# First layers of a gated hybrid decoder step in another order, and two of them by seven products of quarters for eight

## The chip, the cores and the metric

The kernel runs on one core of a Trainium2 chip. The metric is the device time of one execution in microseconds, the median of the runs shown.

## What is computed

One step of a one-layer decoder trunk: a chunked gMLP mixer and a sparse attention mixer side by side, merged by sigmoid gates, then layer norm, a mixture of experts and another layer norm. There are 1024 prompt tokens and 8 sample tokens, 1032 columns in all, each of width 1024. The change touches the projections from x and the first branch:

```python
u, v, q, *kv_new, g_nsa, g_a, g_b = split_projection(xp, w_in[l])
vn = layer_norm(gelu(v), ln_g, ln_b)                 # v, in chunks of 128 positions
a = gelu(u) * (einsum(tril(w_s), vn) + b_s)          # per group of 128 channels
mix = (sigmoid(g_a) * (a @ w_pa) + sigmoid(g_b) * (o @ w_pb)) @ w_o
```

u, v, q, g_a and g_b are 1024 x 1024 layers over the 1032 columns; a @ w_pa (branch a) is one more.

## The kernel before

All values are fp32. A product is made of three passes (`PASSES`, line 184): each operand is split into a high part of the rounded type fp32r and a low part, the rest, and high x high, high x low and low x high are summed in PSUM. The split is always one cast on ACT (`high`) and one subtraction on DVE (`low`).

A 1024 x 1024 layer in turned form is 8 tiles of 128 output channels. A tile (`Tiles.products`, line 245) is 3 thirds of 344 columns x 8 k x 3 passes = 72 matmuls, each of which loads its own 128x128 weights. Its 512 KB of weights are loaded by SP into one of two buffers when the tile before the last is done, then cast by ACT and subtracted by DVE.

The order: `load_and_turn_x` (line 399) loads x in 9 tiles (8 of 128 tokens and the 8 samples), turns each on PE, and casts and subtracts it; the value weights (4 MB) are loaded behind x. `gmlp_values` (line 495) splits the value weights in 8 k, projects v for each token tile (48 matmuls of 512 columns), applies gelu, normalises on DVE (lines 473 to 484), mixes with the turned W_s (`mix(t)`, 8 small matmuls behind the next tile's products) and adds b_s (`keep(t)`) into `m.aT`. At its end PE goes from `mix(7)` to tile 0 of u, and then to `mix(8)`, the samples. `gmlp_gate` (line 652) does u: gelu on ACT, times aT on DVE, and the split of a. `merge_first` (line 706) does the first gate and branch a in turn, 16 tiles. `second_gate` (line 770) does g_b and spills its sigmoid to DRAM (`gate_b`), while the kv weights are loaded and two of their eight k split; `project_kv` and `project_q` follow. Each engine runs its instructions strictly in the order that these functions are called in; what crosses engines waits on semaphores. The lines before the prediction's steps, from `gmlp_values`:

```python
        pe.wait_ge(fw.u.s_lo, 1)
        pe.wait_ge(s_gelu, TT)
        pe.wait_ge(s_kept, TT - 1)
        fw.u.products(0, m.x_parts, 3).then_inc(fw.s_uproj, 1)
        mix(TT)
```

Everything behind the projections (compression, attention, merge, output, router, experts, last norm) is the same in both kernels.

## Time and profile before

| | |
|---|---|
| median of 3 runs | 1965.28 us (1965.21 to 1966.11) |
| the profiled execution's own time | 1966.16 us |
| its span in the trace | 1964.4 us |
| PE busy | 96% of the span |
| DVE, ACT, POOL busy | 54%, 44%, 24% |
| granted TensorE clock, mean | 0.976 |

The span is what the trace covers of one execution; the time is 1.8 us longer, which lies around it. PE stands for TensorE's matmuls, PEld for its weight loads (beside PE), DVE for VectorE, ACT for ScalarE, POOL for GpSimd, SP for the queue that issues the transfers. A busy share is an average over stages; what an engine waits for is read in the stage itself. A matmul's duration is longer than the distance to the next one, since they are pipelined; what a matmul costs is that distance.

### The profile page before, as it was taken

How to read it: one execution, taken by the hardware profiler on the slowest of the kernel's cores; microseconds unless marked ns; L12 is line 12 of the kernel's file. 1: busy time of each engine (PE TensorE's matmuls, PEld its weight loads, DVE VectorE, ACT ScalarE, POOL GpSimd, SP SyncE). 2: the span in 40 equal slices, each digit the busy share in tenths (PEclk: the TensorE clock that was granted, in tenths of full speed). 3: DMA queues.
4: the chain of work that ended last, by engine and by line, in shares of the span. 5: the costliest groups of instructions: out<-in, count | busy, mean ns of one | idle time of the engine just before them, and what ended most of it. 6: DMA issues, size and time to landing. Idle time of an engine off the chain costs nothing.

```text
span 1964.4 us, 31223 instructions
## 1 busy us (share of the span) xinstructions
PE 1886.6 (96%) x11538; PEld 1700.4 (87%) x11539; DVE 1065.5 (54%) x1530; ACT 862.0 (44%) x1455; POOL 467.1 (24%) x640
## 2 busy tenths in 40 slices
PE   7999999999999999999999999999977999999996
PEld 5889999999999987898888988998856888888883
DVE  5543211101112347888888888744557587644756
ACT  4112211112211256778877887520022576544754
POOL 0000000000000025545555554101211244322433
PEclk9999999999999987999999999999987999999998
DMA  6011111132213410000000000434153798877864
GB/s 225 1 33 45 46 52 43 49 117 86 92 39 85 132 35 9 1 1 2 1 1 1 2 1 2 153 95 152 78 201 131 270 390 295 305 276 236 320 205 181
DMA packets 98516, 215.65 MB, mean 110 GB/s; under 512 B 23130, under 2 KB 71810, under 8 KB 92226
## 3 DMA queue, kind: packets, MB, share of 16 engines
q1 hardware_dynamic: 90946, 188.90, 26.7%
q0 software_dynamic: 7456, 25.17, 5.2%
q8 instruction: 79, 1.29, 0.3%
q14 instruction: 35, 0.29, 0.0%
HBM read 181.88 MB, written 34.26 MB: 110 GB/s over the span
## 4 chain that ended last, share of the span: by engine, by line
PE 51%; DVE 6%; ACT 3%; issue 2%; POOL 1%; DVEq 0%; ACTq 0%; POOLq 0%
PE ps L2562 20%; PE ps L1652 6%; PE ps L2233 5%; PE ps L1631 4%; PE ps L251 3%; PE ps L1606 2%; PE ps L1608 2%; DVE small L1706 1%; PE ps L2550 1%; ACT region_w L1795 1%; DVE region L1738 1%; PE ps L2602 1%; PE ps L1598 1%; PE ps L1585 1%; PE ps L2219 1%
## 5 line engine op out<-in xcount | busy, mean ns | idle before, releaser
L1706 DVE TENSOR_REDUCE small<-ps 128x1 f32<-128x640 f32 (+7 forms) x256 | 180.0, 704 | 44.6 <-PE ps L1598 42.0
L1806 ACT CAST turned_high<-ps 128x512 fp32r<-128x512 f32 (+2 forms) x304 | 154.7, 531 | 86.4 <-PE ps L1631 85.9
L1730 DVE TENSOR_TENSOR turned_low<-ps,turned_high 128x512 fp32r<-128x512 f32 (+2 forms) x304 | 173.4, 613 | 8.9 <-ACT turned_high L1806 8.4
L1864 POOL TENSOR_SCALAR region_w<-region_w,small,gates 128x640 f32<-128x640 f32 (+7 forms) x172 | 133.3, 785 | 166.3 <-DVE small L1710 165.8
L1652 PE MATMUL ps<-turned_high,value_stacks 128*128 128x256 f32 (+1 forms) x608 | 152.6, 286 | 10.5 <-DVE region L1738 10.4
L1606 PE MATMUL ps<-key_stacks,query_stacks 128*128 128x256 f32 (+3 forms) x384 | 142.7, 372 | 6.4 <-ACT region L1795 2.3
L2562 PE MATMUL ps<-down_parts,hidden_parts 128*128 128x512 f32 x576 | 139.6, 399 | 3.5 <-DVE down_parts L2858 3.5
L1652 PE MATMUL ps<-turned_low,value_stacks 128*128 128x256 f32 (+1 forms) x608 | 142.6, 279 | 0.0
L2562 PE MATMUL ps<-gate_parts,rows_parts 128*128 128x512 f32 x552 | 133.2, 397 | 3.1 <-DVE rows_parts L2870 3.1
L2562 PEld LDWEIGHTS ps<-down_parts,hidden_parts 128*128 128x128 f32 x576 | 108.5, 192 | 25.4 <-DVE down_parts L2858 3.7
L1652 PEld LDWEIGHTS ps<-turned_high,value_stacks 128*128 128x128 f32 x608 | 115.4, 190 | 16.4 <-issue 15.2
L2562 PE MATMUL ps<-up_parts,rows_parts 128*128 128x512 f32 x552 | 128.9, 389 | 0.0
L1126 POOL MEMSET region<- 128x1096 f32 x1 | 1.1, 1098 | 534.7 <-issue 534.7
L1795 ACT ACTIVATE region_w<-ps,small 128x640 f32<-128x640 f32 (+7 forms) x172 | 121.7, 708 | 10.6 <-DVE small L1706 7.2
L2562 PEld LDWEIGHTS ps<-gate_parts,rows_parts 128*128 128x128 f32 x552 | 103.3, 191 | 24.3 <-issue 3.3
L1608 PE MATMUL ps<-key_lows,query_stacks 128*128 128x256 f32 (+3 forms) x384 | 122.7, 331 | 0.0
L2562 PEld LDWEIGHTS ps<-up_parts,rows_parts 128*128 128x128 f32 x552 | 103.6, 188 | 21.5
L1652 PEld LDWEIGHTS ps<-turned_low,value_stacks 128*128 128x128 f32 x608 | 115.4, 190 | 0.0
L1631 PE MATMUL ps<-ident,region_w 128*128 128x128 f32 x708 | 107.0, 278 | 3.9 <-POOL region_w L1864 3.5
L2233 PE MATMUL ps<-w_out_high,y_parts 128*128 128x512 f32 (+1 forms) x288 | 91.0, 392 | 0.0
L2858 DVE TENSOR_TENSOR down_parts<-region_w,down_parts 128x2048 fp32r<-128x2048 f32 x32 | 72.0, 2289 | 33.9 <-ACT down_parts L2667 32.5
L2858 DVE TENSOR_TENSOR gate_parts<-region_k,gate_parts 128x2048 fp32r<-128x2048 f32 x32 | 71.9, 2288 | 31.4 <-ACT gate_parts L2667 31.4
(466 smaller groups left out, 4983.5 us busy)
## 6 DMA issues: line engine op xcount, KB each, us to landing
region_k<-in_w_gate SPq DMA_DIRECT2D x16, 2048.0 KB, 9.0
region_k<-in_w_up SPq DMA_DIRECT2D x16, 2048.0 KB
region_w<-in_w_down SPq DMA_DIRECT2D x16, 2048.0 KB, 12.8
region_w<-in_w_in SPq DMA_DIRECT2D x20, 512.0 KB, 3.9
gate_b<-region_w SPq DMA_DIRECT2D x8, 516.0 KB, 4.2
region_w<-gate_b SPq DMA_DIRECT2D x8, 516.0 KB, 4.1
region_k<-in_x_prompt SPq DMA_DIRECT2D x8, 512.0 KB, 6.7
region_w<-in_w_in SPq DMA_DIRECT2D x4, 1024.0 KB, 14.3
```

The source lines that it names most:

```text
L1606: nc.tensor.matmul(out, qs[:, g, tile], k1[:, a, g, k0:k0 + w], start=True, stop=False, skip_group_check=True)
L1608: nc.tensor.matmul(out, qs[:, g, tile], k2[a][:, g, k0:k0 + w], start=False, stop=True, skip_group_check=True)
L1631: last = nc.tensor.transpose(m.ps[:, turn_bank(G), r * P:(r + 1) * P], part, m.ident[:])
L1652: last = nc.tensor.matmul(out, vs[:, a, g, b, :], parts[x][:, r * P:r * P + w], start=(a == 0 and r == 0 and x == 0), stop=False, skip_gro ...
L1706: nc.vector.tensor_reduce(nmax[:, n % 4:n % 4 + 1], sc, AX.X, ALU.max, negate=True).then_inc(s_max, 1)
L1730: nc.vector.tensor_tensor(lo, m.ps[:, turn_bank(G), 0:w], hi, ALU.subtract).then_inc(s_lo, 1)
L1795: nc.scalar.activation(probs(H, t), sc, ACT.Exp, bias=nmax[:, n % 4:n % 4 + 1], accum_out=sums[:, H % 4, t:t + 1]).then_inc(s_exp, 1)
L1806: nc.scalar.copy(hi, m.ps[:, turn_bank(G), 0:w]).then_inc(s_hi, 1)
L1864: nc.gpsimd.tensor_scalar(probs(H, t), probs(H, t), rec[:, H % 4, t:t + 1], m.gates[:, 2 * p + t, col:col + 1], ALU.mult, ALU.mult).then_i ...
L2233: last = nc.tensor.matmul(m.ps[0:n, 2 * (t % 2) + c, :], yparts[:, t % 2, a, k, 0:n], wparts[b][:, k, c * 512:(c + 1) * 512], start=(k == ...
L2562: last = nc.tensor.matmul(out, x[:, a, k, :], w[:, b, k, columns], start=(k == 0 and i == 0), stop=(k == count - 1 and i == 2))
L2858: nc.vector.tensor_tensor(wparts[q][:, 1, part], raw_third(m, q)[:, part], wparts[q][:, 0, part], ALU.subtract).then_inc(s_lo[q], 1)
```

## The change

*Order.* The first gate g_a comes first (`first_gate`): its tile 0 is done by thirds between the turnings of x (when three, six and nine x tiles are split; PE turns one tile more before each of the first two), and its sigmoid is spilled to DRAM (`gate_a`). Then u and g_b (`second_layers`), gelu(u) spilled too (`gelu_u`), then the values. `gmlp_values` now reads gelu(u) back per token tile, multiplies it in `keep(t)`, splits a in 8 pieces (`PIECES`: four of the first third of the columns, two each of the second and third; `high_a`, `low_a`), and ends with branch a's tiles 0 and 1 by thirds. `merge_first` is the rest of branch a, with the first gate read back. The second gate's stage is gone, and with it the work beside which the kv weights were loaded and split.

*Seven products.* u and g_b are 8 rounds; round r makes output tiles q and q + 4 of a layer. Weights and x are taken as 2 x 2 quarters: A11, A12, A21, A22 are 512 x 128 of weights, x11 to x22 are 512 x 516 of x. With S1 = A21 + A22, S2 = S1 - A11, S3 = A11 - A21, S4 = A12 - S2 and t1 = x12 - x11, t2 = x22 - t1, t3 = x22 - x12, t4 = x21 - t2, the products are 1 A11 x11, 2 A12 x21, 3 S4 x22, 4 A22 t4, 5 S1 t1, 6 S2 t2, 7 S3 t3, and the four quarters of the output are 1+2, 1+6+5+3, 1+6+7+4 and 1+6+7+5. A product is 4 k x 3 passes x 2 halves of 258 columns = 24 matmuls; two in turn have the same weights. Sums of products with the same bank are made in PSUM, the others by an ACT copy and a DVE addition. The sums of x are made once on DVE beside the first gate; those of the weights in each round (`combine`).

The core of the diff:

```diff
+    def combine(self, dve, r):
+
+        a11, a12, a21, a22, s1, s2, s4 = (self.raw[r % 2][:, q] for q in range(7))
+        for i in range(2):
+            dve.wait_ge(self.s_in[r % 2][i], 16 * (r // 2 + 1))
+        self.sum(dve, s1, a21, a22, ALU.add)
+        self.sum(dve, a21, a11, a21, ALU.subtract)
+        self.sum(dve, s2, s1, a11, ALU.subtract)
+        self.sum(dve, s4, a12, s2, ALU.subtract)
 
...
+        def first_chunk(c):
+            if c == 0:
+                pe.wait_ge(w.s_lo, 1)
+            pe.wait_ge(s_kept, FIRST_TURNS[c] + 1)
+            last = w.chunk(0, m.x_parts, c, c)
+            if c == NC3 - 1:
+                last.then_inc(s_proj, 1)
...
+            if t - 1 in FIRST_TURNS:
+                first_chunk(FIRST_TURNS.index(t - 1))
+        first_chunk(NC3 - 1)
+        for n in range(1, LAYERS):
+            pe.wait_ge(w.s_lo, n + 1)
+            if n >= 2:
+                pe.wait_ge(s_func, n - 1)
+            w.products(n, m.x_parts, 4 * (n % 2)).then_inc(s_proj, 1)
...
+        for n in range(1, LAYERS):
+            w.low(dve, n)
+            if n == 1:
+                dve.wait_ge(fw.s_stack, 2)
+                fw.sums.sum3(dve)
+            if n == 2:
+                fw.sums.sum2(dve)
+                fw.sums.low(dve, fw.sums.t3, fw.sums.raw3, 1)
+            if n == 3:
+                fw.sums.sum4(dve)
+                fw.sums.low(dve, fw.sums.t2, fw.sums.raw2, 2)
+            if n == 4:
+                fw.sums.sum1(dve)
+            if n == 5:
+                fw.sums.low(dve, fw.sums.t4, fw.sums.raw4, 3)
+                fw.sums.low(dve, fw.sums.t1, fw.sums.raw1, 4)
+            if n == 6:
+                fw.half.combine(dve, 0)
+                fw.half.low(dve, 0, 0)
...
+    order = [("1", 0)]
+    for r in range(NR):
+        order += [("2", r), ("6", r), ("5", r), ("7", r)] + ([("1", r + 1)] if r + 1 < NR else []) + [("3", r), ("4", r)]
...
+        def out(done, r, dst, src, sem):
+            sp.wait_ge(done, r + 1)
+            sp.dma_start(dst, src).then_inc(sem, 16)
+
+        for r in range(NR):
+            dst, q = spills[r // HK], r % HK
+            if r == 0:
+                for b in range(2):
+                    sp.wait_ge(fw.s_spill[b], 16 * KT // 2)
+                sp.wait_ge(fw.s_xproj, KT)
+                fw.load_half(sp, 1)
+            elif r + 1 < NR:
+                sp.wait_ge(s_prod, nth["4", r - 1])
+                fw.load_half(sp, r + 1)
+            else:
+                sp.wait_ge(s_prod, nth["4", r - 1])
+                for i in range(3):
+                    fw.load_v(sp, i)
+            out(s_f11, r, dst[q][:, left], first, s_o11)
+            out(s_f22, r, dst[q + HK][:, right], third, s_o22)
+            if r + 1 == NR:
+                sp.wait_ge(s_o22, 16 * NR)
+                fw.load_v(sp, 3)
+            out(s_f12, r, dst[q][:, right], second, s_o12)
+            out(s_f21, r, dst[q + HK][:, left], fourth, s_o21)
...
+            for k in range(HK):
+                for i, (a, b) in enumerate(PASSES):
+                    stationary = (w.hi, w.lo)[a][r % 2][:, q, k, :]
+                    for c in range(2):
+                        last = nc.tensor.matmul(m.ps[:, bank + c, 0:HW // 2], stationary,
+                                                x[b][:, k, c * (HW // 2):(c + 1) * (HW // 2)],
+                                                start=(start and k == 0 and i == 0), stop=(stop and k == HK - 1 and i == 2),
+                                                skip_group_check=True)
+            last.then_inc(s_prod, 1)
...
+        product1(0)
+        for r in range(NR):
+            if r == 0:
+                pe.wait_ge(fw.s_xfunc, KT)
+                pe.wait_ge(x.s_low, 4)
+            else:
+                pe.wait_ge(s_11, r)
+            product("2", r, BANK_C, A12, x.x21, True, True)
+            pe.wait_ge(w.s_lo, 2 * r + 2)
+            pe.wait_ge(s_c1, r + 1)
+            product("6", r, bank_a(r), S2, x.t2, False, False)
+            if r >= 1:
+                pe.wait_ge(s_12, r)
+            product("5", r, BANK_B, S1, x.t1, True, False)
+            pe.wait_ge(s_c2, r + 1)
+            product("7", r, bank_a(r), S3, x.t3, False, False)
+            if r + 1 < NR:
+                product1(r + 1)
+            pe.wait_ge(s_22, r + 1)
+            product("3", r, BANK_B, S4, x.x22, False, True)
+            pe.wait_ge(s_c3, r + 1)
+            product("4", r, bank_a(r), A22, x.t4, False, True)
...
+        w.high(act, 0, 1)
+        keep(0, "1", first, s_c1, s_o11)
+        for r in range(NR):
+            if r + 1 < NR:
+                w.high(act, r + 1, 0)
+            apply(r, s_11, first, s_f11)
+            keep(r, "6", second, s_c2, s_o12)
+            if r + 1 == NR:
+                for k in range(2):
+                    fw.high_v(act, k, nth["5", r])
+            keep(r, "7", third, s_c3, s_o22)
+            if r + 1 < NR:
+                w.high(act, r + 1, 1)
+                keep(r + 1, "1", first, s_c1, s_o11)
+            apply(r, s_22, third, s_f22)
+            if r + 1 == NR:
+                for k in range(2, 4):
+                    fw.high_v(act, k, nth["5", r])
+            apply(r, s_12, second, s_f12)
+            act.wait_ge(s_prod, nth["4", r])
+            if r >= 1:
+                act.wait_ge(s_o21, 16 * r)
+            nc.scalar.activation(halves(fourth), two(bank_a(r)), funcs[r // HK]).then_inc(s_f21, 1)
+        for k in range(4, KT):
+            fw.high_v(act, k, nth["5", NR - 1])
...
+        w.low(dve, 0, 1)
+        for r in range(NR):
+            add(r, "2", s_c1, first, BANK_C, s_11)
+            if r + 1 < NR:
+                w.combine(dve, r + 1)
+                w.low(dve, r + 1, 0)
+            else:
+                for k in range(2):
+                    fw.low_v(dve, k)
+            add(r, "5", s_c3, third, BANK_B, s_22)
+            if r + 1 == NR:
+                for k in range(2, 4):
+                    fw.low_v(dve, k)
+            add(r, "3", s_c2, second, BANK_B, s_12)
+            if r + 1 < NR:
+                w.low(dve, r + 1, 1)
+        for k in range(4, KT):
+            fw.low_v(dve, k)
...
+            if t >= 1:
+                sp.wait_ge(s_gated, t)
+            sp.dma_start(gu[:, :, 0:rows_of(t)], m.gu_dram.rearrange("k p c -> p k c")[:, :, span(t)]).then_inc(s_u, 16)
...
         def turn_ws():
             pe.wait_ge(s_c, 80)
+            pe.wait_ge(fw.s_hfunc[1], NR)
...
-        pe.wait_ge(fw.u.s_lo, 1)
+        pe.wait_ge(w.s_lo, 1)
         pe.wait_ge(s_gelu, TT)
+        pe.wait_ge(s_rows, 1)
+        for c in range(2):
+            for k in range(KT):
+                pe.wait_ge(fw.s_al, k // 2 + 1 if c == 0 else 5 + k // 4)
+                w.term(0, m.a_parts, c, k, c)
+        mix(TT)
+        pe.wait_ge(w.s_lo, 2)
         pe.wait_ge(s_kept, TT - 1)
-        fw.u.products(0, m.x_parts, 3).then_inc(fw.s_uproj, 1)
-        mix(TT)
+        for c in range(2):
+            w.chunk(1, m.a_parts, c, 3 + c)
+        pe.wait_ge(fw.s_al, 8)
+        for n in range(2):
+            w.chunk(n, m.a_parts, 2, 3 * n + 2).then_inc(fw.s_fproj, 1)
...
             nc.vector.tensor_tensor(m.aT[:, :, span(t)], src, add, ALU.add).then_inc(s_kept, 1)
+            dve.wait_ge(s_u, 16 * (t + 1))
+            dve.wait_ge(s_kept, t + 1)
+            nc.vector.tensor_tensor(m.aT[:, :, span(t)], m.aT[:, :, span(t)], gu[:, :, 0:n], ALU.mult).then_inc(s_gated, 1)
...
             if t == TT:
+                for n in range(2):
+                    low_a(dve, n)
                 dve.wait_ge(s_lows, 1)
                 v = vn[t].rearrange("p (a c) -> p a c", a=2)
                 nc.vector.tensor_tensor(v, v, m.ps[0:NB, 0:2, :], ALU.add).then_inc(s_rows, 1)
+                for n in range(2, 4):
+                    low_a(dve, n)
+                keep(TT - 1)
             dve.wait_ge(s_gelu, t + 1)
             normalise(nc, dve, vn[t], rows_of(t), stats, mv, rstd, gain, bias,
                       s_stat, s_mv, s_rstd, s_norm, t, s_v)
...
+            if t == TT:
+                for n in range(4, 6):
+                    low_a(dve, n)
+                w.low(dve, 1)
         keep(TT)
...
+        sp.wait_ge(fw.s_vmix, TT)
+        fw.load_a(sp, 1)
+        sp.wait_ge(fw.s_vnormal, NT9)
+        sp.wait_ge(fw.s_vgated, NT9)
+        sp.dma_start(sa, m.sga_dram[0]).then_inc(s_gate, 16)
+        sp.wait_ge(fw.s_vout, 16)
+        for k in range(4):
+            fw.load_kv(sp, k)
+        for n in range(2, KT):
+            sp.wait_ge(s_proj, n - 1)
+            fw.load_a(sp, n)
...
 
 
     @block.sync
     def _(sp):
-        sp.wait_ge(fw.s_gbproj, KT - 1)
+        sp.wait_ge(fw.s_fproj, KT)
+        for k in range(4, KT):
+            fw.load_kv(sp, k)
         fw.load_q(sp, 0)
...
```

What stands on DVE in a round. Before, in the second gate's and in u's tile, DVE had one subtraction of weights a tile (`gb_low` or `u_low`; u also its multiplication and a's subtraction):

```order
L696 TENSOR_TENSOR region<-region,region_k 128x1032
L698 TENSOR_TENSOR a_low<-region,a_high 128x1032
L243 TENSOR_TENSOR u_low_83<-small,u_high_82 128x1024
L696 TENSOR_TENSOR region<-region,region_k 128x1032
L698 TENSOR_TENSOR a_low<-region,a_high 128x1032
```

Now, one round (line 837 adds products 2, 5 and 3, line 373 combines the next round's weights, line 367 makes their low parts, first of A11 and A12, then of the five others):

```order
L837 TENSOR_TENSOR small<-small,ps 128x516
L373 TENSOR_TENSOR region_w<-region_w 128x512 x4
L367 TENSOR_TENSOR half_w_low_119<-region_w,half_w_high_117 128x1024
L837 TENSOR_TENSOR region_k<-region_k,ps 128x516
L837 TENSOR_TENSOR small<-small,ps 128x516
L367 TENSOR_TENSOR half_w_low_119<-region_w,half_w_high_117 128x2560
```

The combination is between product 2 of this round and product 1 of the next.

The second place is DVE at the end of the value stage (the normalisation of the samples is the six rows from BN_STATS on 8 partitions). Before:

```order
L640 TENSOR_TENSOR region_k<-region_k,ps 8x1024
L475 BN_STATS small<-region_k 8x6
L476 BN_STATS small<-region_k 8x6
L478 BN_AGGR small<-small 8x2
L480 TENSOR_SCALAR region_k<-region_k,small 8x1024
L482 TENSOR_TENSOR region_k<-region_k 8x1024
L484 TENSOR_TENSOR region_k<-region_k 8x1024
L634 TENSOR_TENSOR region<-ps,region_k 128x8x128
L243 TENSOR_TENSOR u_low_85<-region_w,u_high_84 128x1024
L634 TENSOR_TENSOR region<-ps,region_k 128x8x8
```

Now, from a's first pieces (`a_low`, line 914) on:

```order
L914 TENSOR_TENSOR a_low<-region,a_high 128x2x344 x2
L1063 TENSOR_TENSOR region_w<-region_w,ps 8x1024
L914 TENSOR_TENSOR a_low<-region,a_high 128x2x344 x2
L1052 TENSOR_TENSOR region<-ps,region_w 128x8x128
L1055 TENSOR_TENSOR region<-region,small 128x8x128
L861 BN_STATS small<-region_w 8x6
L862 BN_STATS small<-region_w 8x6
L864 BN_AGGR small<-small 8x2
L866 TENSOR_SCALAR region_w<-region_w,small 8x1024
L868 TENSOR_TENSOR region_w<-region_w 8x1024
L870 TENSOR_TENSOR region_w<-region_w 8x1024
L914 TENSOR_TENSOR a_low<-region,a_high 128x4x344 x2
```

The pieces of the second third (128x4x344) stand behind `keep(7)` (two rows now) and the samples' normalisation.

## Rows read from the trace of the kernel before

**Rows 1.** The page, part 1: busy us, share, instructions
```profile
PE 1886.6 (96%) x11538; PEld 1700.4 (87%) x11539; DVE 1065.5 (54%) x1530; ACT 862.0 (44%) x1455; POOL 467.1 (24%) x640
```

**Rows 2.** Stretches: us, each engine's busy us, PEclk, DMA share, GB/s
```profile
0.00:24.00 24.00, 10.66 (x72) 9.00 (x73) 11.36 (x13) 12.15 (x15) 2.23 (x14) 0.96 0.93 357
132.00:232.00 100.00, 99.92 (x627) 97.63 (x625) 38.25 (x35) 25.73 (x25) 0.77 (x2) 0.98 0.18 48
232.00:413.00 181.00, 181.00 (x1154) 181.00 (x1153) 30.51 (x25) 28.25 (x27) 0.00 (x0) 1.00 0.17 47
413.00:503.50 90.50, 90.50 (x578) 90.50 (x577) 10.42 (x9) 15.08 (x15) 0.00 (x0) 1.00 0.34 113
```

**Rows 3.** Timeline of PE in attention, a run of 256-column matmuls: start, duration
```profile
1099.82 0.28 PE L1652 MATMUL ps<-turned_high,value_stacks 128*128 128x256 f32 x1
...
1100.40 0.28 PE L1652 MATMUL ps<-turned_low,value_stacks 128*128 128x256 f32 x1
```

**Rows 4.** Timeline of the start
```profile
6.53 1.01 ACT L459 CAST x_high<-ps 128x1024 fp32r<-128x1024 f32 x1 [4.46 <-PE ps L448]
...
8.94 1.07 PE L448 MATMUL ps<-ident,region_k 128*128 128x128 f32 x8 [0.74 <-DVE x_low L467]
...
19.49 0.63 PE L448 MATMUL ps<-ident,small 8*128 8x8 f32 x8 [0.74 <-DVE x_low L467]
...
24.07 0.79 PE L582 MATMUL ps<-w_v_high,x_high 128*128 128x512 f32 x1 [3.95 <-DVE w_v_low L622]
```

**Rows 5.** Stretches around two falls of PE's clock, columns as in rows 2
```profile
24.00:28.00 4.00, 3.93 (x9) 3.14 (x10) 4.00 (x5) 4.00 (x5) 0.00 (x0) 0.50 1.01 317
28.00:32.00 4.00, 4.00 (x17) 3.21 (x16) 3.96 (x4) 2.67 (x3) 0.00 (x0) 0.90 0.84 292
...
152.00:156.00 4.00, 4.00 (x18) 4.00 (x17) 2.88 (x3) 2.00 (x2) 0.00 (x0) 0.61 0.13 38
```

**Rows 6.** Groups by form: busy us, mean ns of one, idle before
```profile
L2858 DVE TENSOR_TENSOR down_parts<-region_w,down_parts 128x2048 fp32r<-128x2048 f32 x32 | 72.0, 2289 | 33.9 <-ACT down_parts L2667 32.5 <-issue 1.3
L2667 ACT CAST down_parts<-region_w 128x2048 fp32r<-128x2048 f32 x32 | 59.4, 1906 | 10.0 <-DMA region_w<-in_w_down 9.2 <-issue 0.3
L2877 DVE TENSOR_TENSOR region<-region,ps 128x512 f32<-128x512 f32 x24 | 16.4, 684 | 37.8 <-PE ps L2562 37.8
L2688 ACT ACTIVATE region<-ps 128x512 f32<-128x512 f32 x24 | 14.3, 597 | 50.1 <-PE ps L2562 39.6 <-PE ps L2627 10.4
L243 DVE TENSOR_TENSOR gb_low<-region_w,gb_high 128x1024 fp32r<-128x1024 f32 x8 | 9.8, 1224 | 63.5 <-ACT gb_high L238 63.5
L238 ACT CAST gb_high<-region_w 128x1024 fp32r<-128x1024 f32 x8 | 8.4, 1050 | 18.0 <-DMA region_w<-in_w_in 18.0
```

**Rows 7.** Single transfers issued at 232.34, 232.77, 137.29, 493.62, 413.36: us to landing
```profile
region_w<-in_w_in SPq DMA_DIRECT2D x1, 512.0 KB, 4.0
...
region_w<-in_w_in SPq DMA_DIRECT2D x1, 512.0 KB, 5.3
...
region_w<-in_w_branch_a SPq DMA_DIRECT2D x1, 512.0 KB, 6.5
...
gate_b<-region_w SPq DMA_DIRECT2D x1, 516.0 KB, 2.7
...
region<-in_w_in SPq DMA_DIRECT2D x1, 1632.0 KB, 6.5
```

**Rows 8.** Timeline at the value stage's end
```profile
136.03 1.95 PE L563 MATMUL ps<-region_k 128*128 128x128 f32 x16
...
137.29 1.06 SPq L233 DMA_DIRECT2D region_w<-in_w_branch_a  x1
...
142.34 0.68 DVE L475 BATCH_NORM_STATS2 small<-region_k 8x6 f32<-8x512 f32 x1 [3.86 <-ACT region_k L613]
...
146.89 1.21 DVE L484 TENSOR_TENSOR region_k<-region_k 8x1024 f32<-8x1024 f32 x1
```

**Rows 9.** A stretch at the attention's beginning, columns as in rows 2
```profile
725.00:730.00 5.00, 5.00 (x25) 4.78 (x24) 4.89 (x5) 3.30 (x6) 0.00 (x0) 0.50 0.00 0
```

669 lines of the change are left out of this document (374 added, 295 removed).

## The prediction

> **What bounds the kernel now.** I read the page first: PE is busy 96% of the span [rows 1], so time is won by giving PE less to do or by closing its gaps. Then the table of stretches [rows 2]: the layers that the change touches lie between 24 and 504 us, and PE is busy without a break in 132:232, 232:413 and 413:503.5. 1152 of the 344-column matmuls (16 tiles of 72) fill 232:413, 181.0 us, so one costs 157.1 ns. DVE and ACT have 10 to 38 us of work in each of these stretches: they are cover. The start is a gap: 24 us with PE busy for 10.66. Next I read the start's order [rows 4], the durations of the two helpers [rows 6], the landings [rows 7], the tail of the value stage [rows 8] and PE's clock [rows 5, 9].
>
> **The change, part by part.**
>
> *Columns.* Layers u and the second gate are 16 of the 344-column tiles, 1152 matmuls, 181.0 us. Seven products of 24 matmuls in 8 rounds are 1344 matmuls of 258 columns. No row has 258; a run of six matmuls of 256 columns has five steps in 0.58 us, 116 ns each [rows 3], with two columns more 117, and from the 344-column side 157.1 less 86 columns at 2.4 GHz is 121.3 ns. I take 119.5, between the two: 160.6 us. Ends: 157.2 and 163.0. **-20.4 us** (-23.8 to -18.0).
> There are 192 matmuls more, so the part of a matmul's cost that does not shrink with its columns decides: rows 2 and 3 together (41 ns for 88 columns, 37 at 2.4 GHz) leave 9 to 14 ns for it. The Trainium skill (TensorE: Matmul & The Clock Gate, Back-to-back issue gap) gives about 81 ns at 128 columns and 131 at 512 for a stream of weight loads and matmuls, a far larger fixed part: on its line this term would be +6 us.
>
> *Start.* Before, PE turns x until 20.1, then waits for split value weights; its first product starts at 24.07 [rows 4] and runs at 1.2 GHz until about 28.8 (granted 0.50 in 24:28, 0.90 in 28:32 [rows 5]), so 2.4 us more are lost: effectively it starts at 26.4. Now a third of the first gate's tile 0 follows once three x tiles are split. x tile 0 is split on ACT from 6.53 [rows 4]; one weight load lies between x tiles 0 and 1, with one cast (1.05) and one subtraction (1.22) [rows 6]. With the tile's cycle of 1.76 us (turn 1.07, cast 1.01, subtract 1.22, two banks): third one 12.5 to 16.3, second 20.9 to 24.7, last 28.2 to 32.0. A tile is 72 x 0.157 = 11.3 us, so the effective start is 20.7: **-5.7 us** (-6 to -3, the low end if the clock falls here as it did at 20:24).
> The other seven gate tiles run back to back if low(n) is there in 11.3 us: landing 4.0, cast 1.05, cast of a 2064-column sum 1.9, subtraction 2.3, low 1.2, in all 10.5 [rows 6, 7]. Nothing added, 0.8 us of slack.
>
> *First round.* The 2560-column split starts only after the last sigmoid (1.0): cast 2.36, subtraction 2.82 (from 2048 columns in 1.91 and 2.29 [rows 6]) end at 6.3 us; products 1 and 2 cover 5.75. Then ACT is blocked by the cast of weights 1, which are loaded after the last gate spill (4.0 us) and land at 9.3; with a table load and two copies, product 7 waits 0.9. **+1.4** (0.5 to 3).
>
> *Middle rounds.* This is the tightest place. From the end of product 4, which frees a buffer, to the product 1 that reads what is then loaded into it, products 2, 6, 5 and 7 pass: 4 x 24 x 0.1195 = 11.5 us. Against it: fourth activation 0.6, two issues after a spill 0.4, landing of the second of two loads 5.7 (the pair at 232: second issued 0.43 later, 5.3 to land [rows 7]), 0.3 behind the spill's data, four sums of 512 columns 0.69 each, a subtraction of 1024 columns 1.22: 11.1. **0** (up to +0.5 in each of 6 rounds, +3).
>
> *Last round.* No product 1 stands between 7 and 3: product 3 waits for copy 7 (0.6) and addition 5 (0.7): **+1.4**. The value weights are split beside it: the first two before product 3, four more pairs of cast and subtraction within 6.6 us of its end, while PE takes 1.4 us for each k of value tile 0 (6 matmuls of 512, 157 plus 168 columns at 2.4 GHz, 0.227 each), so they are hidden; if they weren't, up to +2. The mixing weights and constants are loaded only when the last spill is out (0.6 + 2.3 us), 4.0 for the first and 1.3 for each of three more: at 11.0, when tile 0 is over at 10.9. **+0.3** (0 to 3).
>
> *Value tail: the dearest added wait.* Zero is the start of mix(7), 136.03 before [rows 8]. Then u tile 0 followed without a gap, since it needs only x. Now branch a follows, which needs a. PE waits for the sample rows (after two casts, two subtractions and the addition: 3.85) from 1.95: 1.9 us. The first third is done at 7.6. The second third needs a pieces 4 and 5, and DVE does these behind keep(7) (two passes of 1.22, to 8.0) and the samples' normalisation, 142.34 to 148.10, 5.76 us [rows 8], though only 8 rows: 13.8, plus a 1376-column subtraction 1.6 = 15.4. PE idles 7.8 us. All else in this tile is in time. Such an idle stretch also costs clock: before, after 3.9 idle us, it ran at 0.50 for 4.7 busy us, 2.4 us lost [rows 4, 5]. 1.9 + 7.8 + 2.4 = **+12.1 us** (8 to 14).
>
> *Branch a, third tile.* Its load waits for the first of the two last chunks; landing 3.9, cast, subtraction 6.2 against a chunk of 3.8: **+2.5** (1.5 to 4). Later tiles have 11.3 us for it.
>
> *kv weights.* Before, all eight k were loaded and two of them split beside the second gate, and PE waited 0.7 us at its end. Now k 4 to 7 are loaded after the last a tile: 4.5 us for the first pair (one of 1632 KB took 6.5 [rows 7], half of it counts some 2 us less), cast, subtraction: 6.6 against 4.6: **+1.4** (0 to 3).
>
> The projections of kv and q, and all behind them, are as before. Branch a's 8 tiles, the gate's 8 and the value tiles have the same matmuls.
>
> Sum: -20.4 - 5.7 + 1.4 + 0 + 1.4 + 0.3 + 12.1 + 2.5 + 1.4 = **-7.0 us**. The profiled execution took 1966.16, so 1959.2 on its own terms. The median of the three runs is 0.9 lower than it: I predict **1958.3**. A measurement of this kernel can tell about 0.2%, 3.9 us, from no change.
>
> **Rivals.**
> *The rounds wait for weights (0.14), which ends on the other side.* Place: DVE's combination of the next round's weights, ahead of product 1, in the six middle rounds. For: 0.4 us of slack only. With three loads queued before, the third took 6.5 from its own issue and 7.5 from the first [rows 7, 8], and its issue alone took SP 1.06 for 0.4 [rows 8]; two spills of 258 KB precede the pair now. With 7.5 for 6.0, 0.6 more for the issue and 0.8 for 0.69 a sum, the chain is 13.6 against 11.5: six times 2.1 are +12.6 on the forecast, 1970.9. It decides from 1.2 us a round. Against: a spill of 516 KB behind nothing landed in 2.7 [rows 7], so its data are short.
> *The clock moves elsewhere (0.15, half to either side).* The attention's beginning runs at 0.50 with PE mostly busy [rows 9], from 721 to 759; nothing in the code fixes its ends, and all of it shifts. A stretch like that in 152:156 (0.61 over 4 us [rows 5], 1.6 us lost) more or less is the smallest step; three of them make it 1953.5 or 1963.
> *The tail is cheaper (0.09).* The clock does not fall, and DVE gets to piece 4 earlier than I count, or the waits at a's third tile and at kv are covered: 4 + 2 + 1.4 less, 1951.
> *A matmul's fixed part is larger than rows 3 show (0.01).* Runs of 256 columns are short there, and here two matmuls in turn have the same weights, each with its own load. At 134.7 ns for 258 columns (181.0 / 1344) the columns give nothing; at 140 they cost 7.2: 1986. Against: both widths measured differ by the clock's price of their columns. The skill's line (the section named above) gives 98 ns for 258 and 109 for 344, by which the whole would be 1984.7; rows 2 and 3 have 157 for 344 and speak against it.
> That the change doesn't do what it says: seven products are in the code, each with its own weight load; no matmul is dropped elsewhere.
>
> **How the numbers follow.** Forecast 0.61, of which 0.10 ends within 0.2%. Of the rounds' 0.14, 0.06 are slower, 0.07 within and 0.01 faster; the clock 0.07 within, 0.08 faster; the tail 0.09 faster; the fixed part 0.01 slower. Faster 0.51 + 0.01 + 0.08 + 0.09 = 0.69, same 0.10 + 0.07 + 0.07 = 0.24, slower 0.07. The bounds of the columns (-3.4 to +2.4), the tail (-4 to +2), start (+2.6), rounds (+3) and constants (+2.7) don't all fall on one side: 1949 to 1968.
>
> **What would show it.** Matmuls of 258 columns start 0.1195 us apart; PE starts its first 344-column matmul at 12 to 13 us; each middle round is 20.1 us with no wait for the weights' low parts; PE idle for 7 to 8 us in the second third of branch a's first tile, released by DVE's a_low, and 0.5 in the clock behind it; 2.5 us before a's third tile; about 2 us in kv tile 0. I am wrong if the rounds take over 21 us, if the tail pause is missing, or if the attention's half-rate stretch changes by more than 7 us.

## The result, and the profile after

The changed kernel takes **1971.12 us** (median of 13 runs, 1966.62 to 1976.28), the kernel before 1965.6 in 13 runs beside them (1963.05 to 1967.85): ratio **1.0029**, 95% interval 1.0020 to 1.0039. It is slower by 5.5 us; 7.0 less was forecast, and the range ended at 1968. Its runs also spread over 10 us instead of 5. The profiled execution took 1972.23 (span 1970.1), 6.1 more than that of before.

The page, part 1, of the changed kernel, answers [rows 1]:

```profile
PE 1873.3 (95%) x11730; PEld 1683.7 (85%) x11731; DVE 1147.1 (58%) x1601; ACT 898.1 (46%) x1502; POOL 471.1 (24%) x640
```

PE has 13 us less to do than before in 192 more matmuls, and the span is 6 longer: what was saved came back as waiting. The stretches say where (columns as in [rows 2]; first gate, seven products, values, tail, branch a, kv and q, compression):

```profile
31.00:112.40 81.40, 81.40 (x520) 81.40 (x519) 42.45 (x25) 21.76 (x18) 0.00 (x0) 1.00 0.32 98
112.40:279.40 167.00, 163.42 (x1346) 162.17 (x1345) 71.07 (x71) 64.22 (x77) 0.00 (x0) 1.00 0.38 118
279.40:397.00 117.60, 113.86 (x554) 92.14 (x553) 63.70 (x72) 17.69 (x19) 7.48 (x17) 0.99 0.22 66
397.00:435.00 38.00, 27.26 (x160) 26.48 (x160) 19.31 (x20) 9.04 (x9) 0.76 (x2) 0.91 0.37 113
435.00:503.30 68.30, 68.01 (x433) 68.01 (x434) 15.49 (x14) 6.90 (x7) 0.00 (x0) 1.00 0.26 81
503.30:666.30 163.00, 161.16 (x957) 157.33 (x957) 32.61 (x40) 24.26 (x33) 0.00 (x0) 1.00 0.28 79
666.30:739.80 73.50, 66.93 (x409) 60.80 (x407) 33.19 (x92) 32.49 (x73) 11.32 (x21) 0.89 0.29 87
```

PE's rows that carry a wait, in brackets the idle time and its releaser (timeline of PE):

```profile
118.82 0.52 PE L757 MATMUL ps<-x_sum_high,half_w_high 128*128 128x258 f32 x2 [0.42 <-DVE half_w_low L367]
...
273.56 0.51 PE L757 MATMUL ps<-x_high,half_w_high 128*128 128x258 f32 x2 [1.48 <-DVE region_k L837]
...
293.37 1.29 PE L953 MATMUL ps<-ident,region_w 128*128 128x128 f32 x8 [2.57 <-DMA small<-in_gmlp_ws]
...
398.04 0.40 PE L250 MATMUL ps<-a_high,branch_a_high 128*128 128x344 f32 x1 [2.21 <-DVE region_w L1063]
409.06 0.66 PE L250 MATMUL ps<-a_high,branch_a_high 128*128 128x344 f32 x1 [7.01 <-DVE a_low L914]
435.29 0.43 PE L250 MATMUL ps<-a_high,branch_a_high 128*128 128x344 f32 x1 [2.98 <-DVE branch_a_low L244]
...
510.00 0.45 PE L1205 MATMUL ps<-w_kv_high,x_high 128*128 128x408 f32 x1 [1.74 <-DVE w_kv_low L459]
...
710.44 3.61 PE L1472 MATMUL ps<-ident,region 128*128 128x128 f32 x16 [2.65 <-DMA region<-in_cache_kv]
```

All but the last lie where the change altered the code or the order of the loads. Three of the waits are followed by a stretch in which PE's clock is granted 0.50, though PE is busy again (the stretch with the wait, then the one behind it; before each the clock is at 1.00 or 0.99):

```profile
291.00:294.10 3.10, 0.73 (x7) 0.73 (x8) 0.00 (x0) 0.86 (x1) 0.00 (x0) 1.00 1.00 347
294.10:297.50 3.40, 3.40 (x12) 2.72 (x11) 2.75 (x5) 0.00 (x0) 1.11 (x1) 0.50 0.02 5
402.00:406.80 4.80, 0.05 (x1) 0.00 (x0) 3.73 (x6) 0.00 (x0) 0.76 (x2) 1.00 0.12 7
406.80:413.60 6.80, 4.54 (x16) 4.54 (x17) 4.24 (x4) 1.04 (x1) 0.00 (x0) 0.50 0.30 82
707.50:710.60 3.10, 0.45 (x3) 0.16 (x2) 0.00 (x0) 0.46 (x1) 0.00 (x0) 0.99 0.26 83
710.60:714.00 3.40, 3.40 (x17) 3.40 (x17) 1.39 (x2) 0.59 (x1) 0.00 (x0) 0.51 0.00 0
```

They cost 1.6, 2.2 and 1.6 us beyond the waits (each step in them less the median step of its shape at full rate). No such stretch follows the waits of 2.21 us at 398.04 and of 2.98 at 435.29, so the length of a wait alone doesn't tell whether the clock falls.

The last wait is in compression, the stage behind q, code that the change does not touch. Before, the same turn of the keys starts with no wait:

```profile
706.58 1.91 PE L1160 MATMUL ps<-ident,region 128*128 128x128 f32 x16
```

PE needs the last of 16 pages there, and SP's loop issues them one by one. SP's issues in that loop, before and after (start, time from the first to the end of the last issue, count):

```profile
685.07 19.25 SPq L395 DMA_DIRECT2D region<-in_cache_kv  x13
```

```profile
685.00 23.61 SPq L532 DMA_DIRECT2D region<-in_cache_kv  x14
```

Less the last issue itself (0.36) that is 12 turns in 18.9 us before and 13 in 23.25 after: **1.58 and 1.79 us a turn**, the same instructions. The transfers themselves land as quickly (2.3 and 2.2 us). A turn is ten instructions of SP, and the extra stands in two of its steps: from the loop's branch to the next instruction 0.27 us for 0.16, and from that one to the next 0.19 for 0.10.

### The profile page after: what moved, and what is told of

It reads as the page before. It is cut to its first block, busy times and chain, and to the rows that moved or that the text cites. A ratio compares the mean times of both kernels' runs of the same rounds, so it can differ in the third digit from the quotient of the medians.

```text
span 1970.1 us, 31853 instructions
## 1 busy us (share of the span) xinstructions
PE 1873.3 (95%) x11730; PEld 1683.7 (85%) x11731; DVE 1147.1 (58%) x1601; ACT 898.1 (46%) x1502; POOL 471.1 (24%) x640
## 4 chain that ended last, share of the span: by engine, by line
PE 45%; DVE 6%; ACT 3%; issue 3%; DMA 3%; POOL 1%; DVEq 0%; ACTq 0%; POOLq 0%; SPq 0%
PE ps L2874 15%; PE ps L1964 6%; PE ps L2545 5%; PE ps L1943 4%; PE ps L250 3%; DMA region_w<-in_w_down 2%; PE ps L1918 2%; PE ps L1920 2%; DVE small L2018 1%; DVE region L2050 1%; PE ps L2914 1%; ACT region_w L2107 1%; PE ps L1910 1%; PE ps L2862 1%; DVE down_parts L3170 1%
## 5 line engine op out<-in xcount | busy, mean ns | idle before, releaser
L1964 PEld LDWEIGHTS ps<-turned_high,value_stacks 128*128 128x128 f32 x608 | 115.4, 190 | 16.5 <-issue 15.3
L3170 DVE TENSOR_TENSOR down_parts<-region_w,down_parts 128x2048 fp32r<-128x2048 f32 x32 | 72.0, 2288 | 34.2 <-ACT down_parts L2979 32.9
L1918 PEld LDWEIGHTS ps<-key_stacks,query_stacks 128*128 128x128 f32 x384 | 74.0, 193 | 14.8 <-issue 9.9
```

What stands on the lines that cost most here:

```text
L1918: nc.tensor.matmul(out, qs[:, g, tile], k1[:, a, g, k0:k0 + w], start=True, stop=False, skip_group_check=True)
L1964: last = nc.tensor.matmul(out, vs[:, a, g, b, :], parts[x][:, r * P:r * P + w], start=(a == 0 and r == 0 and x == 0), stop=False, skip_gro ...
L3170: nc.vector.tensor_tensor(wparts[q][:, 1, part], raw_third(m, q)[:, part], wparts[q][:, 0, part], ALU.subtract).then_inc(s_lo[q], 1)
```

## The experiments

Each was compared with the kernel before on the same chip, but not all on one chip. Ratios are therefore compared, not medians. The difference of two ratios is uncertain by about 0.15%, 3 us (an estimate from the two intervals). Medians and ratios:

| kernel | median us (runs) | ratio to before, 95% |
|---|---|---|
| changed | 1971.12 (13) | 1.0029 (1.0020 to 1.0039) |
| changed, once more (e11_changed_again) | 1974.43 (5) | 1.0043 (1.0030 to 1.0056) |
| low first (e1_low_first) | 1976.85 (6) | 1.0064 (1.0052 to 1.0076) |
| tail (e2_tail) | 1967.12 (12) | 1.0012 (1.0000 to 1.0023) |
| constants (e3_consts) | 1970.93 (7) | 1.0029 (1.0018 to 1.0041) |
| loop head (e4_head16) | 1968.33 (12) | 1.0017 (1.0006 to 1.0028) |
| tail + constants (e9_tail_consts) | 1963.72 (11) | 0.9989 (0.9978 to 0.9999) |
| tail + head (e10_tail_head) | 1961.63 (12) | 0.9982 (0.9972 to 0.9992) |
| all three (e5_all) | 1958.25 (5) | 0.9963 (0.9950 to 0.9977) |
| all three, more (e8_more) | 1958.65 (5) | 0.9965 (0.9952 to 0.9979) |
| the same, product 4 first (e12_four_first) | 1957.29 (7) | 0.9967 (0.9951 to 0.9983) |
| order without seven products (e6_plain) | 1977.71 (4) | 1.0064 (1.0048 to 1.0079) |
| before, SP padded (e7_before_pad) | 1969.02 (10) | 1.0022 (1.0012 to 1.0031) |

**1. Is the page loop slower because of where it lies?** Two runs from opposite sides. In the changed kernel the loop's head is pinned:

```diff
-    with sp.Fori(first, end) as i:
+    with m.nc.Fori(first, end, engines=bass.OrderedEngineSet([sp.engine]),
+                   head_slot=head and {sp.engine: head}) as i:
...
-            load_pages(m, io, sp, m.R1, slice(256, 512), 4096, si.s_page)
+            load_pages(m, io, sp, m.R1, slice(256, 512), 4096, si.s_page, head=16)
```

> Only the place in memory of SyncE's loop over the 16 page loads of the compress stage is changed: its first instruction is put at a fixed slot (16) of an instruction block; the instructions are the same. In the kernel before a turn of this loop takes 1.58 us, in the changed one 1.79, with the extra 0.21 us in the two steps right behind the loop's branch. Theory A (placement of the loop's head, moved by the extra SyncE instructions of the change): a turn takes 1.5 to 1.6 us, the last page lands 3 us earlier, TensorE's 2.8 us wait at 707.5 and the half-rate stretch behind it (1.6 us) go, time 1966 to 1968. Theory B (contention, or the page table read): a turn stays at 1.79 us and the time at 1971.

In the kernel before, 55 idle instructions push it on:

```diff
+        for i in range(55):
+            sp.nop(f"pad{i}")
         sp.wait_ge(s_xl, 1)
```

> The kernel before with 55 idle SyncE instructions (as many as the change adds to SyncE ahead of that point) put where SyncE waits anyway, ahead of the page loop; nothing else. If the place of the loop's head in memory makes a turn 1.79 instead of 1.58 us: the last page lands 3 us later than in the kernel before, TensorE waits 2.6 to 3 us at about 706, the clock falls behind it, and the time is 3 to 5 us above before (1968 to 1970). Rival: the loop keeps its 1.58 us (what slowed it is something else that the change does), time as before.

SP's issues, pinned (changed kernel) and padded (kernel before):

```profile
686.88 24.05 SPq L532 DMA_DIRECT2D region<-in_cache_kv  x16
```

```profile
682.30 25.83 SPq L395 DMA_DIRECT2D region<-in_cache_kv  x15
```

Pinned: 23.7 / 15 = 1.58 us a turn, and PE turns the keys at 713.10 with no wait. Padded: 25.47 / 14 = 1.82 (the extra stands at the branch, 0.28 for 0.16, and behind the read of the page's number, 0.30 for 0.20), and the wait is there in the kernel before:

```profile
709.92 1.96 PE L1162 MATMUL ps<-ident,region 128*128 128x128 f32 x16 [3.14 <-DMA region<-in_cache_kv]
```

By the ratios the padded kernel is 0.22% (4.3 us) slower than before, clear of 1 by its interval. The pinned one is 2.4 us faster than the changed one (5.1 against its second series), and the first of these is within the uncertainty. Its profiled execution shows why so little is seen: from kv's start to the end it takes 1461.6 us, the changed kernel 1466.8, but kv starts 5.1 us later (508.37 for 503.28), with more stretches at half rate ahead of it, in code that is the same (part 3 has them).

That the place of the loop sets its turn is shown from both sides, and contention as the cause of the slower turn is out: the pinned kernel issues the same transfers. Counted in the traces, SP runs 264 instructions ahead of the loop in the kernel before and 303 in the one without seven products (part 5), both with the fast turn, and 319 in the padded and 321 in the changed one, both with the slow turn. The pinned one has 322 and the fast turn: not the number as such, but where it puts the loop. Which boundary the loop meets is not shown. The Trainium skill (Runtime: NRT & Kernel Launch, Instruction fetch mechanics) says that most engines fetch instructions in blocks of 256 and hold two, and that a taken branch to code outside them has to wait for a fetch. No run here tells whether the 0.2 us a turn is such a wait.

**2. The tail: one order, two ways.** First VectorE's order alone:

```diff
-                for n in range(2, 4):
+                for n in range(2, 6):
                     low_a(dve, n)
                 keep(TT - 1)
...
-                for n in range(4, 6):
-                    low_a(dve, n)
                 w.low(dve, 1)
```

> VectorE writes pieces 4 and 5 of a_low (first two of the second 344-column third) before it adds and gates value tile 7; nothing else changes. In the changed kernel TensorE waits 7.2 us for piece 4. Theory A (the wait is VectorE's queue, and it is passed on): piece 4 lands near 401.7 us, so that wait goes, but normalising the sample rows ends no earlier than before (the same 13 us of VectorE work stand ahead of it), and the mix of the sample rows, which is next on TensorE, waits 6 to 7 us instead; start of the key-value products 503.3 us within 1 us, time within 0.2% of the changed kernel's 1971. Theory B (the wait is piece 4 alone): the mix does not wait, the half-rate stretch at 407 goes too, time 1962 to 1964.

PE's next wait, and the clock behind it:

```profile
412.46 3.58 PE L968 MATMUL ps<-small,region_w 8*128 8x8 f32 x16 [5.62 <-DVE region_w L870]
419.50 0.65 PE L250 MATMUL ps<-a_high,branch_a_high 128*128 128x344 f32 x1 [3.46 <-DVE branch_a_low L244]
```

```profile
411.50:425.10 13.60, 9.18 (x35) 9.09 (x36) 5.58 (x6) 3.62 (x3) 0.00 (x0) 0.50 0.45 134
```

The wait was handed on, as theory A says: 5.6 us at the mix of the sample rows. But a second one followed it, 3.5 for the second weight tile, which the changed kernel doesn't have: 9.1 us of waiting instead of 7.0. PE was at half rate for 13.6 us instead of 6.8 (how much of that is this execution's own is open, see part 3), and kv starts at 508.38, not at 503.3. The kernel is 0.35% slower than the changed one (0.21% against its second series). Both theories missed that.

Then the order of all four queues:

```diff
+            if t == TT:
+                sp.wait_ge(s_mix, TT)
+                fw.load_a(sp, 1)
             if t >= 1:
                 sp.wait_ge(s_gated, t)
...
-        mix(TT)
         pe.wait_ge(w.s_lo, 2)
         pe.wait_ge(s_kept, TT - 1)
-        for c in range(2):
-            w.chunk(1, m.a_parts, c, 3 + c)
+        w.chunk(1, m.a_parts, 0, 3)
+        mix(TT)
+        w.chunk(1, m.a_parts, 1, 4)
...
-                keep(TT - 1)
             dve.wait_ge(s_gelu, t + 1)
-            normalise(nc, dve, vn[t], rows_of(t), ...)
+            moments(nc, dve, vn[t], rows_of(t), ...)
+            if t == TT:
+                for n in range(4, 6):
+                    low_a(dve, n)
+                w.low(dve, 1)
+            scale(nc, dve, vn[t], rows_of(t), ...)
...
+        keep(TT - 1)
         keep(TT)
```

`moments` and `scale` are the two halves of `normalise`, cut ahead of its wait for GpSimd's deviation; the load of a's second tile stood behind the sample rows' output.

> The end of the value stage in another order: branch a's second weight tile is loaded as soon as the mix of tile 7 is done, ahead of the wait for the sample rows; VectorE takes the moments of the sample rows, then a_low pieces 4 and 5 and the weight tile's low part, then scales the rows; TensorE puts the first third of the second tile ahead of the mix of the sample rows and the second third behind it. If the tail's waits are what the trace says (7.2 + 2.2 of half rate, TensorE idle with work that could run), 6 to 9 us of it go: start of the key-value products 494 to 497 us instead of 503.3, and the time 1962 to 1965. Rival: whatever the tail gives back is lost behind it, since the page loads of the compress stage set the start of attention; then the wait there grows and the time stays within 0.2% of 1971.

The 7.0 us wait is gone, 1.8 remain at another place (and 3.4 us at half rate behind it):

```profile
421.01 0.43 PE L250 MATMUL ps<-a_high,branch_a_high 128*128 128x344 f32 x1 [1.77 <-DVE a_low L918]
```

In this execution the values began 2.8 us later than in the changed kernel's (282.21 for 279.46). Half of that is a fall of PE's clock in the first gate, behind a wait of 1.91 us that the changed kernel has too, there without a fall:

```profile
29.30:32.70 3.40, 3.06 (x11) 3.07 (x12) 3.37 (x5) 1.51 (x2) 0.00 (x0) 0.51 0.00 0
```

Kv starts at 501.19, not at 494 to 497 as expected: 4.8 us are won between. By the ratios the time fell by 3.3 us (6.1 against the second series). The rival is out: the wait in compression is 2.9 us, for 2.7 in the changed kernel.

**3. The constants.**

```diff
-        for out in fw.s_hout:
-            sp.wait_ge(out, 16 * NR)
-        sp.dma_start(ws, io["gmlp_ws"].rearrange("l g t s -> t (l g) s")).then_inc(s_c, 16)
+        sp.wait_ge(fw.s_hprod, 7 * NR)
+        sp.dma_start(ws, io["gmlp_ws"].rearrange("l g t s -> t (l g) s")).then_inc(s_ws_in, 16)
...
+        for out in fw.s_hout:
+            sp.wait_ge(out, 16 * NR)
         with nc.allow_non_contiguous_dma(reason="one weight per group"):
...
-            pe.wait_ge(s_c, 80)
+            pe.wait_ge(s_ws_in, 16)
```

> The mixing weights, gain, bias and spatial bias are loaded as soon as the last of the seven-product rounds is done (about 279.5 us) instead of behind the four spills (284.8), and TensorE's turn of the mixing weights waits for their load alone, not for all five constants. If the 2.7 us wait at 290.6 and the half-rate stretch 294.1 to 297.5 (1.6 us) come from these loads: both go, value tile 1 starts near 291.5 instead of 294.3 and runs at full rate, time 1966 to 1967.5. Rival: the clock stretch does not come from the wait and stays (time 1968.5), or the load is late anyway because the last piece of the value weights is in the queues (wait stays over 1.5 us, time 1970).

The wait and the fall of the clock at 294 are gone, as expected:

```profile
290.00:296.00 6.00, 6.00 (x32) 4.99 (x31) 2.27 (x4) 1.02 (x1) 0.98 (x1) 1.00 0.54 188
```

Yet by the ratios the time is that of the changed kernel's first series (and 2.8 us below its second). In the profiled execution the tail has three stretches at half rate, where the changed kernel's has one:

```profile
395.70:399.10 3.40, 3.40 (x12) 3.40 (x13) 3.30 (x4) 3.29 (x3) 0.00 (x0) 0.50 0.00 0
405.90:412.70 6.80, 6.00 (x21) 6.00 (x22) 3.47 (x3) 1.05 (x1) 0.00 (x0) 0.50 0.29 82
416.20:419.60 3.40, 3.40 (x14) 3.40 (x13) 2.26 (x2) 2.35 (x2) 0.00 (x0) 0.50 0.77 243
```

It would be easy to read this as the clock taking back what the edit gave. But the pinned kernel's profile has three stretches in the same place too, at 408.9, 419.1 and 439.6, and its code is the changed kernel's up to there:

```profile
419.10:422.50 3.40, 3.40 (x13) 3.40 (x14) 1.89 (x3) 2.58 (x2) 0.00 (x0) 0.50 0.50 151
439.60:443.00 3.40, 3.40 (x14) 3.40 (x14) 1.55 (x2) 1.05 (x1) 0.00 (x0) 0.50 0.51 166
```

How often the clock falls in the tail thus varies from execution to execution, and one profile of each kernel can't say that the constants' edit caused it. From the start of the values to kv this execution takes 221.6 us, the two profiled ones of the changed kernel 223.8 and 223.7.

**4. Do the three add?** The pairs and the triple.

> The reordered tail and the early constants, the page loop left where the change puts it. Alone, the tail was worth 3.3 us of median, the constants nothing and the loop's place 2.4, but all three together 13. Theory A (two idle stretches close to each other draw the clock down further, so the constants pay only when the tail's waits are gone): 1962 to 1963.5, that is the three together less the 4.4 us of the page loop's wait and its half-rate stretch. Theory B (the three are independent, and the sum of all was a draw of the clock): 1967 to 1968.

> The reordered tail and the page loop's head at slot 16, the constants left as in the changed kernel. Theory A (as for the run before): the constants' wait (2.7) and its half-rate stretch (1.6) are back, and with them falls of the clock behind them: 1962 to 1964.5. Theory B: 1965.5, the sum of the two alone.

> The changed kernel once more, unchanged, on the same chip and against the same runs of the kernel before as the two runs above, for the spread: 1966 to 1976 with a median of 1971, 0.3% above before. If it comes out below 1968, the comparisons with it across chips have to be read with that.

> The three edits that each left work order intact but for one place, together: the reordered end of the value stage, the mixing weights loaded early, the page loop's head at slot 16. If their gains add: against the changed kernel's 1971.1, 4 us (tail) and 2.5 to 3 us (loop) and 0 to 4 us (constants; alone it removed the wait but the clock fell elsewhere): 1961 to 1965, level with or below the kernel before (1965). Rival: the clock takes back what the waits give; then the trace shows more than three half-rate stretches between 290 and 450 us and the time stays at 1966 to 1968.

The pairs came out at 1963.7 and 1961.6, where theory B had 1967 to 1968 and 1965.5. But theory B's figures rest on the first series of the changed kernel (1.0029). With the second (1.0043), a plain sum of the single edits gives 0.9998 and 0.9986 for the pairs and 0.9972 for all three, and the measured 0.9989, 0.9982 and 0.9963 have these within their intervals. So it is **not shown whether the three add**; the first series alone says that they give more together.

By the ratios the constants are worth 4.5 us once the tail is in order and 3.7 with the loop pinned too; on the tail as the change made it, between nothing and 2.8. The loop's place is worth 5.9 on the tail's kernel, 5.1 on tail and constants. What doesn't hang on these differences is the whole: all three are 7.3 us faster than the kernel before (0.9963, interval 0.9950 to 0.9977) and 13 faster than the changed kernel. In its profiled execution kv starts at 496.80 and the rest takes 1459.7 us (before: 503.67 and 1460.7; changed: 503.28 and 1466.8). The second series of the changed kernel came out higher, 1.0043; what is told here against the changed kernel uses the first unless said.

**5. The two halves of the change.**

```diff
-LAYERS = KT
+LAYERS = 3 * KT
...
-        col = COL_GA + n * P
+        col = (COL_GA, 0, COL_GB)[n // KT] + n % KT * P
...
-            second_layers(nc, m, io, fw, block)
```

> The new order without the seven products: u and the second gate come from sixteen more plain 344-column weight tiles (1152 products) in the same loop as the first gate, still ahead of the values; all behind is as in the changed kernel. This prices the two halves of the change apart. From the traces: sixteen tiles at 11.3 us are 181, the seven-product stage took 167.0, so this kernel should be 12 to 16 us slower than the changed one (1983 to 1987), the order alone 18 to 22 us worse than before, and the seven products worth about 14. Rival: the waits at the end of the seven-product stage and the constants' wait belong to the seven products and go with them; then 7 to 9 us slower (1978 to 1980).

In its profiled execution the values start at 294.72 instead of 279.46 and kv at 514.94 instead of 503.28 (before: 503.67). So **the order alone costs some 11 us by the start of kv, and the seven products give some 11 back** (both some 10 without the 1.3 that PE's slower start took in this execution, see the last section): 15.3 up to the values, less 3.6 behind them, mostly the constants (a wait of 2.7 is 1.3 here, with no fall of the clock behind it). This kernel also loads and splits the value weights in another place, beside the last four of its tiles. The median is only 6.6 above the changed kernel, below both expectations: SP has another number of instructions here, the page loop runs at 1.57 us a turn, and the 4.4 us behind it are absent. With them added (an estimate) it would be 11, still below the 12 to 16 that were expected.

**6. Two smaller places, then a third.**

```diff
             if r + 1 < NR:
                 w.combine(dve, r + 1)
                 w.low(dve, r + 1, 0)
-            else:
-                for k in range(2):
-                    fw.low_v(dve, k)
             add(r, "5", s_c3, third, BANK_B, s_22)
             if r + 1 == NR:
-                for k in range(2, 4):
+                for k in range(4):
                     fw.low_v(dve, k)
...
-                for n in range(2):
-                    high_a(act, n)
                 nc.scalar.copy(dst, m.ps[32:32 + NB, 2 * b:2 * b + 2, :]).then_inc(s_lows, 1)
-                for n in range(2, 4):
+                for n in range(4):
                     high_a(act, n)
```

VectorE's `low_a(0)` and `low_a(1)` go behind its addition of the rows in the same way.

> e5_all and two more places: in the last seven-product round VectorE adds product 5 ahead of the low parts of two value weight pieces (TensorE waits 1.6 us for that sum now), and ScalarE copies the sample rows ahead of the first four pieces of a_high, VectorE adds them ahead of the first two of a_low (TensorE waits 2.4 us for them now). Expected 1.6 and 0.7 us less than e5_all: 1959 to 1963. Rival: the value weights' low parts then come late and TensorE waits in the first value tile instead, time as e5_all.

PE's wait in the last round did not move, so VectorE's order was not its cause:

```profile
274.26 0.51 PE L757 MATMUL ps<-x_high,half_w_high 128*128 128x258 f32 x2 [1.48 <-DVE region_k L837]
```

The rows' wait fell from 2.2 to 1.4 us, but a second one appeared behind it, so that PE waits 2.6 us in all and nothing is won:

```profile
393.56 0.40 PE L250 MATMUL ps<-a_high,branch_a_high 128*128 128x344 f32 x1 [1.43 <-DVE a_low L916]
398.70 0.42 PE L250 MATMUL ps<-a_high,branch_a_high 128*128 128x344 f32 x1 [1.14 <-DVE a_low L916]
```

The time is that of all three. Then products 3 and 4 of the last round were exchanged:

```diff
-        order += [...] + [("3", r), ("4", r)]
+        order += [...] + ([("3", r), ("4", r)] if r + 1 < NR else [("4", r), ("3", r)])
```

> e8_more with the last two products of the last round exchanged, so that TensorE takes the one that waits only for ScalarE's copy while VectorE adds. Its 1.64 us wait in the last round did not answer to VectorE's order in e8_more: it is the chain product 7, copy, addition, product 3, with no first product of a next round to run meanwhile. Expected: a wait of 0.7 us instead of 1.6, time 0.5 to 1 us below e8_more (1957.5 to 1958.5). Rival: the wait moves to the value tile that waits for the last round's sums, time as e8_more (1958.7).

```profile
274.34 0.51 PE L757 MATMUL ps<-x_sum_high,half_w_high 128*128 128x258 f32 x2 [0.68 <-ACT region_k L803]
```

The wait fell from 1.5 to 0.7 us, as the chain product, copy, addition, product says. The median is the lowest of all, 1957.29, but its interval overlaps those of both kernels above it: no gain is shown.

## Why the prediction was wrong, step by step

Against the profiled execution of before, up to the start of kv (-8.4 forecast, -0.4 measured: 503.67 to 503.28):

| step | forecast | measured | how |
|---|---|---|---|
| columns | -20.4 | -19.2 | 167.0 us of stage less 5.2 of waits, for 181.0 |
| start | -5.7 | -4.4 | the rounds start at 112.46: less 8 x 11.31 is 22.0, for 26.4 |
| rounds (first, middle, last) | +2.8 | +5.2 | steps above the median of 120 ns |
| constants | +0.3 | +4.3 | wait 2.7, half rate 1.6 |
| value tail | +12.1 | +11.9 | 2.4 + 7.3 + 2.2 |
| third tile | +2.5 | +3.1 | |
| fall of the clock at 152 before | not counted | -1.8 | [rows 5] |

The rest, 0.5, is mostly the value tiles, 12.95 us each for 12.90.

**Right.** The matmul of 258 columns: a product's steps are 120 ns apart, 119.5 was forecast. These rows, two matmuls each, are 0.25 us apart (0.24 in the median):

```profile
180.84 0.41 PE L757 MATMUL ps<-x_sum_high,half_w_high 128*128 128x258 f32 x2
181.09 0.41 PE L757 MATMUL ps<-x_sum_low,half_w_high 128*128 128x258 f32 x2
```

The Trainium skill's line (TensorE: Matmul & The Clock Gate, Back-to-back issue gap) gives about 98 for them and 109 for 344 columns (estimates, on a line between its two figures), where this case has 120 and 157; the measured ones decide. The tail's 12.1 was right to 0.2, in part by luck: of its three parts the wait for the rows was 0.5 longer, the wait for piece 4 0.5 shorter, the half rate behind it 0.2 less. The third tile and the kv weights (+1.4 forecast; the waits in kv's first two tiles are 2.6 us for 1.0 before) were right to 0.6.

**Wrong, the first step that failed: "The projections of kv and q, and all behind them, are as before."** Their code is; their SP queue is not. The page loop costs 0.21 us more in each of 15 turns, the last page lands at 710.39 instead of 706.11, PE had half a microsecond of slack there before, and so it waits 2.8 us and loses 1.6 to the clock. Kv started 0.4 us early and attention 5.3 us late (739.86 for 734.55). Removed alone, this brings the changed kernel to 0.17% above before, about 1969, which is still far from the 1958.3 forecast. In part it was bad luck: with 303 instructions ahead of it the loop keeps its 1.57 us.

**Wrong, the second step: the constants' load, +0.3 forecast and 4.3 measured.** The chain was to end 11.0 us into the values, and PE went on at 13.9 (293.37 less 279.46). Most of the difference is the last spill: 2.3 us were counted for it, and it took 4.4 to land (issued at 280.29, 4.0 us behind a load of value weights of 1024 KB), so that the first constant is issued at 5.3 instead of 2.9. From there it took 8.6 us for 8.1; a fifth transfer, 8 x 8 elements, was not counted. The view names this fifth one as the releaser, but all five count on one semaphore and the DMA engines are full until then (share 1.00), so which landed last is not shown. And behind the wait came 3.4 us at half rate, 1.6 lost, where the forecast charged the clock only for the tail.

**Wrong in size: start and rounds**, 1.3 and 2.4 us. In the rounds it is spread over many small waits: the halves' low parts in several rounds (the middle ones were to have none), 0.9 beside the activation table's load, 1.6 in the last round.

The rivals. "The rounds wait for weights" had the right sign and the wrong place: they lost 5.2, not 15.4. "The clock moves elsewhere" is in part what happened: the spread of 10 us goes with it. In the changed kernel's 13 runs the fastest, 1966.62, has a mean granted clock of 0.977, the slowest, 1976.28, one of 0.974; with the tail's order alone 1962.16 goes with 0.977 and 1972.72 with 0.973. A difference of 0.003 is some 6 us of the span (an estimate), so more than half of the spread.

The sum: -7.0 forecast; +8.0 missed ahead of kv, +0.2 in kv, +4.2 in compression, +0.7 behind it and around the span, gives the 6.1 measured. The parts before kv alone would have made it a draw; the page loop made it slower. The page loop (4.2) and the constants (4.0) are 8.2 of the 13.1 us between forecast and measurement.

## What to carry to other kernels

When an expensive stage is cut, price every place where its order met another queue: here 19 us of columns and 4 of start went into a tail (11.9), rounds (5.2), a constants' load (4.3) and a weight tile (3.1) that the old order had covered, and two edits of order and a pinned loop turned +0.3% into -0.4%. Count a possible 1.6 to 2.2 us of half rate on top of each short wait, and look at what stands behind a wait before moving it: moved alone (low first), it let a second one out and cost more than it did where it was. One profile doesn't show where the clock falls in general: two of the same code differ. And before calling the code behind a change unchanged, look at hand-issued loops there whose last transfer has no slack: instructions added far ahead of them can slow them.

## What was not expected of the hardware

- **A loop's turn on SP depends on where it lies**: 1.57 to 1.60 us in seven kernels, 1.79 in six, 1.82 in the padded one, in each execution the same for nearly all turns. The same loop in the q stage, four turns at a time, ran at 1.50 to 1.54 in both kernels.
- **At the start PE runs at half its pace for longer.** Eight transposes take 1.94 us or 1.06. In the kernel before the switch comes before 8.94 [rows 4]; in the new order, where PE starts with longer gaps, it comes between 10.7 and 12.1 us in the changed kernel's profile, and only after 13.9 in the second. The granted clock reads 1.00 in all of these microseconds, so that this is the clock is inferred from the durations alone:

```profile
11.94 1.94 PE L618 MATMUL ps<-ident,region_k 128*128 128x128 f32 x8 [0.75 <-DVE x_low L661]
```

  There the third third of the first gate's tile 0 starts 1.2 us later (30.59 for 29.39), and the values at 281.58 for 279.46. Eight of the twelve profiled executions of the new order were like the second.
- **The half-rate stretch at attention's start has no fixed length.** Its code is the same in all, and it took 37.6 us of 0.50 in before and changed, 34.2 in all three and in the pinned kernel, 27.3 in both pairs (here tail + head):

```profile
720.20:747.50 27.30, 22.10 (x100) 19.59 (x100) 16.77 (x40) 15.80 (x36) 9.72 (x12) 0.50 0.09 20
```

  What sets it is open; no run was made on it. The two profiled executions with 27.3 us are the fastest of their kernels' (1956.66 for a median of 1963.72, and 1958.83 for 1961.63), so these may not be typical of them.
